# The first block's decay scalars: TensorE takes their small products behind the projections' dense products in each turn, not ahead of them

## The chip, the cores and the metric

The kernel runs on one core of a Trainium2 chip. The metric is the device time of one execution in microseconds (us), the median over timed runs; lower is better. In the rows PE is TensorE (matrix products and transposes), PEld its weight loads, DVE is VectorE, ACT is ScalarE, POOL is GpSimd and SP is SyncE, which issues the transfers.

## The reference, cut to what matters

Two blocks of two layers each work on a sequence of 512 positions and 1024 features. The change concerns the first block, in both of its layers. There a normalised input `h` is projected into attention (q, k, v), into a gated delta rule (qd, kd, vd and two sets of scalars, beta and decay, for 2 directions x 8 heads) and into gates:

```
proj = h @ w_in[l]
(qa, ka, va, qd, kd, vd, beta_logit, decay_logit, z, gate_logit) = jnp.split(proj, offsets, axis=-1)
...
y_attn = grid_attention(qa, ka, va) @ w_o_attn[l]
qkv = jax.nn.silu(centred_depthwise_conv(jnp.concatenate([qd, kd, vd], axis=-1), dn_conv_w[l])).astype(f32)
...
beta = jax.nn.sigmoid(beta_logit.astype(f32)).reshape(b, s, 2, DN_HEADS)
g = -jnp.exp(dn_a_log[l].astype(f32)) * jax.nn.softplus(
    decay_logit.astype(f32).reshape(b, s, 2, DN_HEADS) + dn_dt_bias[l].astype(f32))
o = bidir_gated_deltanet(qd, kd, vd, beta, g)
...
gcum = jnp.cumsum(g, axis=-1)
g_tot = jnp.exp(gcum[..., -1])
```

The "decay scalars" are `g`, its running sums within chunks of 64 (`gcum`) and the exponential of each chunk's total (`g_tot`).

## The kernel before, in words

Every engine has a program of its own, written out in Python: the classes `Tensor` (PE), `Scalar` (ACT), `Vector` (DVE), `Pool` and `Sync` all derive from `Program`. Each engine does its instructions strictly in the order in which its generator emits them, and waits on semaphores for events of the others. The generators of the several strands of work are interleaved by hand: `abreast(a, b, c)` takes one step of each strand in each turn, in the order in which they are given, and `beside(main, fill, 1, 1)` puts one step of `fill` behind every turn of `main`.

`Program.mixed` sets the order of the middle of a layer. Its first stage, which the change touches, interleaves four strands on each engine:

- `scalars`: the small products of the decay scalars. On PE there are three groups. The first, the *scalar transposes* (4 of 32x32, L617), turns the product of `h` with the scalars' weights. The second, the *running sums* (key `cum`, 3 products from `s_scg`), and the third, the *totals* (key `tot`, 4 products from `s_scg`, L852 to L856), work on `g`. DVE takes the first and the second, ACT the third: it writes `s_egt`, the exponential of the totals (L1592).
- `begun` and `project(0, (1,))`: the dense products of the delta rule's q, k and v, two halves each, here called q0, q1, k0, k1, v0, v1 (keys `(l, "p", 0, s3, j)`). One step on PE is half of one, 12 products of 128x512 with `s_h` and `s_whi` or `s_wlo`. On ACT and DVE each of them goes on with a convolution of five taps (ACT writes the middle one into `s_tmp`, DVE adds four more, L1974, two in one step and two in a later one), then a tanh on ACT and a product on DVE (silu). For q and k a square on ACT and a sum of squares over it on PE follow; for k and v, four transposes.
- `fill`: the attention, whose units go score (PE, `s_vtok,s_dno`), row maximum (DVE, `s_nm`), exponential (ACT, `s_x`), two sets of four transposes (PE L700), their copies (DVE and ACT write `s_ktok`) and the product with v (PE, `s_ktok,s_vtok`). The sets of transposes are numbered T0, T1, ...

PSUM has eight banks. Which bank a product takes is decided by a queue in the program, not by the chip:

```
    def take(self, key):
        buffer, free = self.slots.pop(0)
        self.after(free)
...
    def give(self, key, *free):
        buffer = (self.k.bank if isinstance(self, Tensor) else self.k.tmp)[key]
        self.slots.append((buffer, free))
```

`give` puts a bank at the end of the queue, together with the event that will free it; it is called where PE's program has issued the product, long before that event. `take` pops the bank at the head, whichever it is, and makes PE wait for its event. So the order of PE's instructions also decides which product waits for which reader of an earlier one. A dense product gives its bank with the event "last tap of the convolution", which DVE reaches late; the running sums give theirs with the event `kd0`, DVE's subtraction into `s_sckd`.

Of the kernel before, what the change touches and what calls it, by code (L numbers as in the profile page):

```python
# [176 lines left out]
class Program:  # L177
# [72 lines left out]
    def behind(self, mark):  # L250

        while self.made < min(self.k.marks.get(mark, 0) + AHEAD, len(self.k.order)):
            self.one_ahead()
# [11 lines left out]
    def mixed(self, l, attention, scalars, begun, project, gates, plug):  # L265

        units = lambda g: abreast(self.units(l, g, 0), delayed(self.units(l, g, 1), 2))  # L270
        fill = itertools.chain(attention(), project(1, (0, 1)))
        beside(abreast(scalars, begun, delayed(project(0, (1,)), 0)), fill, 1, 1)
        beside(plugged(units(0), plug, (0, 1, 4, 5, 21, 22)), fill, 1, 1)
        beside(plugged(self.chain(l, 0), plug, (0, 1, 4, 5, 8, 9, 12, 13)), fill, 1, 1)
        for _ in fill:
            pass
        fill = gates()
        beside(plugged(units(1), plug, (4, 5, 21, 22)), fill, 5, 4)
        beside(self.chain(l, 1), fill, 5, 4)
        for _ in fill:  # L280
            pass

    def gates_with(self, b, c):


        return () if b == 0 else (c,) if b == 1 else (0, 1) if c == 0 else (c + 1,) if c < 7 else ()

    def project(self, l, g, js, *inputs):

        items = [(l, "p", g, s3, j) for s3 in range(3) for j in js]  # L290
        return overlapped((self.project_begin(key, *inputs), self.project_end(key)) for key in items)
# [17 lines left out]
def together(*parts, lag=0):  # L309

    live = list(parts)
    n = 0
    while live:
        for p in list(live):
            if n < lag * parts.index(p):
                continue
            if next(p, 1) == 1:
                live.remove(p)
        n += 1


def abreast(*parts):

    live = list(parts)
    while live:
        live = [p for p in live if next(p, 1) != 1]
        yield


def beside(main, fill, n, turns):  # L330

    left = 0
    for _ in main:
        left += turns
        while left >= n:
            left -= n
            next(fill, None)
# [10 lines left out]
def plugged(steps, plug, turns):  # L348
    for n, _ in enumerate(steps):
        if n in turns:  # L350
            next(plug, None)
        yield


def delayed(steps, n):
    for _ in range(n):
        yield
    yield from steps


def overlapped(items):

    rest = []
    for head, tail in items:
        for _ in head:
            rest = [p for p in rest if next(p, 1) != 1]
            yield
        rest.append(tail)
    yield from abreast(*rest)
# [137 lines left out]
def grid_attn(m, l):  # L507
    return Attn(lambda p, e, i: m.aq[half(e), p, tile(i)], lambda p, e, n: m.ak[half(e), 0:n],
                lambda p, e, c: m.av[:, c, half(e)], lambda i: 512, False, None, m.aE, m.aPT,
                [("vec_qk", (l, "q", 4), "out")], 0, 0, each=lambda p: ("vec_qk", (l, "q", p), "out"), clear=[("dma_spill", l)], lag=1)  # L510
# [20 lines left out]
class Tensor(Program):  # L531
# [230 lines left out]
    def layer1(self, l):  # L762
        m, d = self.m, self.d
        hi, lo = m.mixh
        wt = d["w1"]
        tag = ("mix", l) if l else "in"
        ht, raw = self.normed(tag), self.unscaled(tag)

        scalars, begun = self.scalars(l, hi, lo, ht), self.project(l, 0, (0,), hi, lo, ht)

        def first(c):
            if c < 6:
                self.lin((l, "q", ORDER_Q[c]) if c < 5 else (l, "v"), wt[l, ORDER_Q[c] if c < 5 else 5], 8, m.raw[:, 0], m.raw[:, 1], raw, amid=(lambda: self.total(tag)) if c == (l == 0) else None)
            elif c == 6:
                next(scalars)
            else:
                next(begun)
                next(begun)

        def rest(c):  # L780
            if c < 5:
                self.qk((l, "q", ORDER_Q[c]), K_BO)
            elif c == 5:
                self.turned((l, "v"))
        for _ in behind(first, rest, 8, LAG):
            pass
        f, A = grid_attn(m, l), ("A", l)

        self.mixed(l, lambda: self.attention(A, f), scalars, begun, lambda g, js: self.project(l, g, js, hi, lo, ht),
                   lambda: itertools.chain(self.gates(l, hi, lo, ht), self.early(l, hi, lo, ht)),  # L790
                   self.plug(l, hi, lo, ht))

        def branch(name, c, gate, w, made, a):
            if name == "a" and c > 4:
                self.lin((l, name, "g", c), wt[l, gate + c], 8, hi, lo, ht)
                self.give((l, name, "g", c), ("act_mix", l, name, c))
            self.lin((l, name, c), d[w][l, c], 4, a[:, 0], a[:, 1], made)
            self.give((l, name, c), ("vec_mix", l, name, c))

        def branch_a():  # L800
            for c in ORDER_A:
                branch("a", c, 22, "woa", lambda k: [("vec_mix", l, "oat", k)], m.orr)
                yield

        def outputs():
            for i in range(4):
                yield
                self.to_features((l, "D"), i, m.o[:, i, :], ("vec_mix", l, "o", i), ("vec_mix", l, "gated", i))
                yield
        together(outputs(), branch_a())  # L810
        for c in range(8):
            branch("d", c, 30, "wod", lambda k: [("vec_mix", l, "od", 3)], m.odr)

        def step(c):
            self.lin((l, "o", c), d["wo1"][l, c], 8, hi, lo, lambda k: [("vec_mix", l, "h", k)])
            self.give((l, "o", c), ("vec_x", l, "mix", c))
        for c in range(8):
            step(c)
        tag = ("ffn", l)
        ht2, raw2 = self.normed(tag), self.unscaled(tag)  # L820
        act = m.ffa
        for n, (f0, nf) in enumerate(FGROUPS):
            for f in range(f0, f0 + nf):
                for half in range(2):
                    if f < RAW:
                        self.lin((l, "up", f, half), d["wup"][l, half * FT + f], 8, m.raw[:, 0], m.raw[:, 1], raw2, amid=(lambda: self.total(tag)) if f + half == 0 else None)
                    else:
                        self.lin((l, "up", f, half), d["wup"][l, half * FT + f], 8, hi, lo, ht2)
                    self.give((l, "up", f, half), ("vec_ffn", l, f, half, "conv"))

            def step(c):
                self.lin((l, "dn", n, c), d["wdn"][l, c][:, f0 * 128:(f0 + nf) * 128], nf, act[:, 0], act[:, 1], lambda k: [("vec_ffn", l, f0 + k, "lo")])
                self.give((l, "dn", n, c), ("vec_x", l, "ffn", n, c))
            for c in range(8):
                step(c)

    def scalars(self, l, hi, lo, ht):
        m, sc = self.m, self.m.sc
# [137 lines left out]
    def units(self, l, g, r):  # L976
        for jp in range(2):
            yield from self.unit(l, g, jp, r)
# [65 lines left out]
    def gates(self, l, hi, lo, ht):  # L1044
        for c in range(4):
            key = (l, "z", c)
            yield from self.lin_steps(key, self.d["w1"][l, 18 + c], 8, hi, lo, ht, 2)
            self.give(key, ("vec_proj", key))
            yield
# [1950 lines left out]
```

How the kernel before makes its waits and increments, by code:

```python
    def wait_ge(self, signal, value):  # L152
        if self.passed.get(id(signal), 0) < value:
            self.passed[id(signal)] = value
            self.e.wait_ge(signal.sem, value)
# [38 lines left out]
    def after(self, events):  # L194
        for event in events:
            self.w.wait_ge(*self.at(*event))
# [340 lines left out]
    def weights(self, key, src, kt, w=128):  # L537
        n = self.used
        self.used += 1
        if self.k.counting:
            self.k.order.append((src, kt, w))
            self.k.number[key] = n
        self.w.wait_ge(*self.at("lo", n))
        return [a[:, 0:kt * w].rearrange("p (k m) -> p k m", k=kt) for a in self.m.half[n % TILES]]
# [48 lines left out]
    def turned(self, key):  # L594
        self.give(key, ("act_attn", *key, "copy"))
        ps = self.take((key, "T"))
        self.w.wait_ge(*self.at("act_attn", *key, "copy"))
        self.turn4(ps, self.tmp((key, "s"))).then_inc(*self.up("pe_feat", *key))
        self.give((key, "T"), ("act_attn", *key))
# [1 line left out]
    def lin_narrow(self, key, src, kt, hi, lo, made, w):  # L602
# [6 lines left out]
            last = self.mm(ps[0:w, :], wlo[:, k, :], hi[:, k, :], False, k == kt - 1)  # L609
        last.then_inc(*self.up("prod", self.used - 1))
        self.give(key, ("act_dn", key, "copy"))
        yield
        ps = self.take((key, "T"))
        self.w.wait_ge(*self.at("act_dn", key, "copy"))
        s = self.tmp((key, "s"))
        for i in range(4):
# [678 lines left out]
    def raw(self, tag):  # L1295
        m = self.m
        n, col, made = self.raws(tag)
        self.w.wait_ge(*self.at("dma_par", n, "row"))
        def square(c):
```

## Time and profile before

| | |
|---|---|
| median of 3 timed runs | 3263.2 us (3262.95 to 3265.39) |
| the profiled execution's own time | 3262.69 us |
| its span, first to last instruction | 3260.8 us |
| PE busy | 3137.0 us, 96% of the span |
| mean granted TensorE clock | 0.993 of full speed |
| the changed stage, layer 0 | about 60 to 141 us of the span |
| the changed stage, layer 1 | about 1010 to 1085 us of the span |

The span is what the trace covers; the profiled execution took 1.9 us more than it, and 0.5 us less than the median of the timed runs. A row of a timeline gives the start in us, the duration in us, the engine, the line, the operation with what it writes and reads, and the number of instructions merged in the row; brackets at its end hold the idle time just ahead of it on that engine, and what ended it.

### The profile page before, as it was taken

What the parts mean: (1) busy time and instruction counts of PE and PEld (TensorE: products, weight loads), DVE (VectorE), ACT (ScalarE), POOL (GpSimd) and SP (SyncE); (2) the same over time, 40 slices, a digit from 0 to 9 for tenths busy, and PEclk for the clock granted to TensorE, in tenths of its full rate; (3) what the DMA queues carried; (4) which work ended last, traced back from release to release, by engine and by line L of the source; (5) the groups of instructions that cost most, each with busy time, mean ns of one, the idle gap of its engine ahead of it and who ended that gap; (6) DMA issues with size and microseconds to landing.
All of it is one profiled execution on the core that took longest, in us unless ns stands there. A gap on an engine that the chain in (4) does not pass through costs nothing.

```text
span 3260.8 us, 59864 instructions
## 1 busy us (share of the span) xinstructions
PE 3137.0 (96%) x25752; PEld 2483.0 (76%) x25752; DVE 1886.1 (58%) x3058; ACT 1394.3 (43%) x2454; POOL 446.7 (14%) x440
## 2 busy tenths in 40 slices
PE   8899999999999999999999999999999999999999
PEld 5687778888876687878888876777788767676887
DVE  6576657756466675656745565554444555635443
ACT  5645224434246544334433355454433454544432
POOL 0051430000000331600000002211200011203010
PEclk9899999999999999999999999999999999999999
DMA  5001103333332011123333232222132232221323
GB/s 177 27 22 47 41 29 123 106 95 97 95 116 81 21 29 54 41 71 112 97 97 96 88 122 99 62 65 72 56 94 74 89 109 69 65 72 58 86 73 100
DMA packets 80215, 255.02 MB, mean 78 GB/s; under 512 B 11344, under 2 KB 13008, under 8 KB 78928
## 3 DMA queue, kind: packets, MB, share of 16 engines
q1 hardware_dynamic: 79952, 251.19, 25.0%
q8 instruction: 204, 3.34, 0.4%
q14 instruction: 59, 0.48, 0.0%
HBM read 238.08 MB, written 6.29 MB: 75 GB/s over the span
## 4 chain that ended last, share of the span: by engine, by line
PE 79%; DVE 9%; ACT 6%; issue 2%; DMA 1%; POOL 1%; SPq 1%; ACTq 0%; DVEq 0%; POOLq 0%
PE psum L535 76%; PE psum L700 3%; DVE s_wlo L1971 2%; DVE s_xb L1971 1%; ACT s_tmp L1273 1%; ACT s_whi L1273 1%; DVE s_tmp L1974 1%; DVE s_ffy L1974 1%; DMA s_stage<-w 1%; POOL s_xb L2690 1%; ACT s_E L1273 1%; ACT L1283 1%; SPq L2838 0%; DVE psum L1971 0%; ACT L1273 0%
## 5 line engine op out<-in xcount | busy, mean ns | idle before, releaser
L535 PE MATMUL psum<-s_h,s_whi 128*128 128x512 f32 (+1 forms) x4576 | 1456.9, 400 | 21.2 <-DVE s_wlo L1971 14.3
L535 PEld LDWEIGHTS psum<-s_h,s_whi 128*128 128x128 f32 (+1 forms) x4576 | 847.2, 189 | 235.2 <-issue 34.8
L535 PE MATMUL psum<-s_h,s_wlo 128*128 128x512 f32 (+1 forms) x2288 | 897.5, 392 | 0.0
L1971 DVE TENSOR_TENSOR s_wlo<-s_stage,s_whi 128x1024 fp32r<-128x1024 f32 (+2 forms) x468 | 533.9, 1143 | 358.5 <-ACT s_whi L1273 357.4
L1273 ACT ACTIVATE s_whi<-s_stage 128x1024 fp32r<-128x1024 f32 (+2 forms) x468 | 450.6, 967 | 261.5 <-DMA s_stage<-w 75.9
L535 PEld LDWEIGHTS psum<-s_h,s_wlo 128*128 128x128 f32 (+1 forms) x2288 | 430.8, 188 | 95.1
L2690 POOL TENSOR_TENSOR s_xb<-s_xb,s_cstm 64x512 f32<-64x512 f32 x64 | 101.1, 1579 | 900.5 <-DVE s_xb L1971 896.3
L535 PE MATMUL psum<-s_ffa,s_whi 128*128 128x512 f32 x704 | 217.5, 390 | 4.6 <-DVE s_ffa L1971 4.6
L1974 DVE SCALAR_TENSOR_TENSOR s_ffy<-psum,s_pcol,s_ffy 128x511 f32<-128x511 f32 x176 | 131.7, 748 | 110.8 <-ACT s_ffy L1273 107.7
L1273 ACT ACTIVATE s_E<-psum,s_nm 128x256 f32<-128x256 f32 (+3 forms) x224 | 114.4, 515 | 186.7 <-DVE s_nm L2057 151.3
L535 PE MATMUL psum<-s_oR,s_whi 128*128 128x512 f32 (+1 forms) x640 | 183.4, 371 | 0.0
L2734 POOL TENSOR_SCALAR s_E<-s_E,s_inv 128x256 f32<-128x256 f32 (+3 forms) x96 | 98.2, 1036 | 495.2 <-DVE s_inv L2079 489.0
L535 PE MATMUL psum<-s_raw,s_whi 128*128 128x512 f32 (+1 forms) x480 | 154.2, 403 | 8.3 <-DVE s_raw L1974 8.3
L535 PEld LDWEIGHTS psum<-s_ffa,s_whi 128*128 128x128 f32 x704 | 131.7, 188 | 34.2 <-DVE s_ffa L1971 7.1
L1974 DVE SCALAR_TENSOR_TENSOR s_x<-psum,s_x 128x512 f32<-128x512 f32 x80 | 55.3, 691 | 165.0 <-PE psum L535 164.9
L1971 DVE TENSOR_TENSOR s_xb<-s_xb,psum 128x512 f32<-128x512 f32 (+1 forms) x176 | 102.4, 630 | 71.6 <-PE psum L535 71.6
L1273 ACT ACTIVATE s_tmp<-psum 128x512 f32<-128x512 f32 (+4 forms) x126 | 70.8, 562 | 170.0 <-PE psum L535 166.0
L535 PE MATMUL psum<-s_ffa,s_wlo 128*128 128x512 f32 x352 | 137.0, 389 | 0.0
L1273 ACT ACTIVATE s_ffy<-psum,s_pcol 128x512 f32<-128x512 f32 x88 | 60.5, 687 | 173.0 <-PE psum L535 157.2
L1273 ACT ACTIVATE s_xb<-psum 128x512 f32<-128x512 f32 x118 | 69.8, 597 | 139.0 <-PE psum L535 139.0
L535 PEld LDWEIGHTS psum<-s_oR,s_whi 128*128 128x128 f32 x640 | 114.4, 189 | 18.7
L535 PEld LDWEIGHTS psum<-s_xb 64*64 64x64 f32 x5632 | 104.5, 134 | 29.9 <-issue 15.0
(310 smaller groups left out, 4348.2 us busy)
## 6 DMA issues: line engine op xcount, KB each, us to landing
s_stage<-w SPq DMA_DIRECT2D x192, 512.0 KB, 3.6
s_stage<-wup SPq DMA_DIRECT2D x88, 512.0 KB, 3.6
s_stage<-wo SPq DMA_DIRECT2D x32, 512.0 KB, 3.6
s_stage<-wdn SPq DMA_DIRECT2D x32, 512.0 KB, 3.5
s_stage<-wdn SPq DMA_DIRECT2D x16, 384.0 KB, 3.1
spill<-s_x SPq DMA_DIRECT2D x2, 2048.0 KB, 8.7
s_stage<-woa SPq DMA_DIRECT2D x16, 256.0 KB, 2.6
s_x<-spill SPq DMA_DIRECT2D x2, 2048.0 KB, 8.0
```

The source lines that it names most:

```text
L535: return self.e.matmul(out, left, right, start=first, stop=last, skip_group_check=True)
L700: last = self.e.transpose(ps[:, tile(c)], f.e(U)[:, tile(c)], m.cst[:, K_ID, :])
L1273: return self.e.activation(out, src, func, **kw)
L1283: self.e.preload_act_table_set("natural_log_exp_and_others")
L1971: return self.e.tensor_tensor(out, a, b, op)
L1974: return self.e.scalar_tensor_tensor(out=out, in0=a, scalar=s, in1=b, op0=op0, op1=op1)
L2690: return self.e.tensor_tensor(out, a, b, op)
L2734: self.e.tensor_scalar(E, E, inv, None, ALU.mult).then_inc(*self.up("pool_attn", tag, "e", U))
```

## The change

Only PE's program changes. In each turn of the first stage of `mixed`, PE takes the step of `scalars` behind the steps of the two dense strands, where it took it ahead of them. The step of the attention still ends the turn. All other engines keep their order.

```diff
         fill = itertools.chain(attention(), project(1, (0, 1)))
-        beside(abreast(scalars, begun, delayed(project(0, (1,)), 0)), fill, 1, 1)
+        beside(abreast(*self.in_turn(scalars, [begun, project(0, (1,))])), fill, 1, 1)
...
+    def in_turn(self, scalars, dense):
+
+        return [scalars] + dense
...
# class Tensor
+    def in_turn(self, scalars, dense):
+
+        return dense + [scalars]
```

In both layers this moves the three small groups on PE, each behind the 12 dense products of its turn. The largest consequence for the order is at the totals. These are PE's rows there before the change, in layer 0, from the last product of attention with v ahead of them (`s_ktok,s_vtok`) on; the eight transposes of L700 are T4 and T5, the four products from `s_scg` are the totals, the rows with `s_h` are the first half of v1, and `s_vtok,s_dno` is the next score:

```order
L535 MATMUL psum<-s_ktok,s_vtok 64x128 x8
L700 MATMUL psum<-s_cst,s_x 128x128 x8
L535 MATMUL psum<-s_scg,s_csta 128x32 x4
L535 MATMUL psum<-s_h,s_whi 128x512 x2
L535 MATMUL psum<-s_h,s_wlo 128x512
L535 MATMUL psum<-s_h,s_whi 128x512 x2
L535 MATMUL psum<-s_h,s_wlo 128x512
L535 MATMUL psum<-s_h,s_whi 128x512 x2
L535 MATMUL psum<-s_h,s_wlo 128x512
L535 MATMUL psum<-s_h,s_whi 128x512 x2
L535 MATMUL psum<-s_h,s_wlo 128x512
L535 MATMUL psum<-s_vtok,s_dno 128x512 x2
```

And these are the same rows of PE after it, where the changed file's lines stand four further down (L539 for L535, L704 for L700):

```order
L539 MATMUL psum<-s_ktok,s_vtok 64x128 x8
L704 MATMUL psum<-s_cst,s_x 128x128 x8
L539 MATMUL psum<-s_h,s_whi 128x512 x2
L539 MATMUL psum<-s_h,s_wlo 128x512
L539 MATMUL psum<-s_h,s_whi 128x512 x2
L539 MATMUL psum<-s_h,s_wlo 128x512
L539 MATMUL psum<-s_h,s_whi 128x512 x2
L539 MATMUL psum<-s_h,s_wlo 128x512
L539 MATMUL psum<-s_h,s_whi 128x512 x2
L539 MATMUL psum<-s_h,s_wlo 128x512
L539 MATMUL psum<-s_scg,s_csta 128x32 x4
L539 MATMUL psum<-s_vtok,s_dno 128x512 x2
```

The totals moved from ahead of the 12 dense products to behind them. The scalar transposes and the running sums move in the same way in earlier turns.

ACT's program is the same before and after. These are its rows from the copy of T5 on (`s_ktok<-psum`), in layer 0, before the change: the totals' exponential, the middle tap of v0 (`s_tmp<-psum,s_pcol`), a cast of weights, a load of a function table, the tanh of k1, its square, another table, two exponentials of the attention and the two steps that make k1's norm from its sum of squares:

```order
L1273 ACTIVATE s_ktok<-psum 128x512
L1273 ACTIVATE s_egt<-psum 128x64
L1273 ACTIVATE s_tmp<-psum,s_pcol 128x512
L1273 ACTIVATE s_whi<-s_stage 128x1024
L1273 ACT_TABLE_LOAD
L1273 ACTIVATE s_tmp<-s_tmp 128x512
L1273 ACTIVATE s_tmp<-s_qkv 128x512
L1283 ACT_TABLE_LOAD
L1273 ACTIVATE s_x,s_rs<-psum,s_nm 128x512 x2
L1273 ACTIVATE s_tmp<-psum,s_eps 128x512
L1273 ACTIVATE s_tmp<-s_tmp 128x512
```

Nothing moved here: the totals' exponential still stands ahead of everything that follows it.

## Rows read from the trace of the kernel before

**Rows 1.** The page's busy time of each engine over the span.

```profile
PE 3137.0 (96%) x25752; PEld 2483.0 (76%) x25752; DVE 1886.1 (58%) x3058; ACT 1394.3 (43%) x2454; POOL 446.7 (14%) x440
```

**Rows 2.** Timeline of PE in layer 0, the changed stage.

```profile
63.62 0.43 PE L617 MATMUL psum<-s_cst,s_tmp 32*128 32x32 f32 x4 [0.40 <-ACT s_tmp L1273]
...
98.63 0.73 PE L535 MATMUL psum<-s_scg,s_csta 128*128 128x32 f32 x4
...
109.56 0.66 PE L700 MATMUL psum<-s_cst,s_x 128*128 128x128 f32 x4 [0.65 <-DVE s_sckd L1971]
112.15 1.45 PE L535 MATMUL psum<-s_scg,s_csta 128*128 128x32 f32 x8 [1.94 <-DVE s_tmp L1974]
...
118.66 0.72 PE L535 MATMUL psum<-s_h,s_whi 128*128 128x512 f32 x2
...
121.53 1.02 PE L535 MATMUL psum<-s_tmp,s_cst 128*128 128x512 f32 x2
...
123.51 1.09 PE L700 MATMUL psum<-s_cst,s_x 128*128 128x128 f32 x8
124.44 0.60 PE L622 MATMUL psum<-s_cst,s_qkv 128*128 128x128 f32 x4
...
128.53 0.63 PE L622 MATMUL psum<-s_cst,s_tmp 128*128 128x128 f32 x4 [2.44 <-DVE s_tmp L1974]
```

**Rows 3.** Timeline of PE in layer 1, the changed stage.

```profile
1012.33 0.43 PE L617 MATMUL psum<-s_cst,s_tmp 32*128 32x32 f32 x4
...
1042.08 0.53 PE L535 MATMUL psum<-s_scg,s_csta 128*128 128x32 f32 x4
...
1042.67 0.70 PE L535 MATMUL psum<-s_h,s_whi 128*128 128x512 f32 x2
...
1056.12 1.91 PE L535 MATMUL psum<-s_scg,s_csta 128*128 128x32 f32 x8 [1.94 <-DVE s_tmp L1974]
```

**Rows 4.** Timeline of DVE in layer 0.

```profile
78.92 0.22 DVE L1974 SCALAR_TENSOR_TENSOR s_scg<-s_schb,s_prow 128x64 f32<-128x64 f32 x1
...
110.57 1.53 DVE L1974 SCALAR_TENSOR_TENSOR s_tmp<-psum,s_pcol,s_tmp 128x511 f32<-128x511 f32 x2
```

**Rows 5.** The chain of work that ended last, from 112 us on: start, duration, what.

```profile
112.15 11.42 PE psum L535 x54
```

**Rows 6.** Timeline of ACT in layer 0, from the totals' exponential on.

```profile
113.64 0.22 ACT L1273 ACTIVATE s_egt<-psum 128x64 f32<-128x64 f32 x1 [1.49 <-PE psum L535]
...
118.38 0.63 ACT L1273 ACTIVATE s_tmp<-s_qkv 128x512 f32<-128x512 f32 x1 [1.05 <-DVE s_qkv L1974]
...
122.59 0.69 ACT L1273 ACTIVATE s_tmp<-psum,s_eps 128x512 f32<-128x512 f32 x1 [0.82 <-PE psum L535]
...
124.64 1.08 ACT L1273 ACTIVATE s_ktok<-psum 128x512 f32<-128x512 f32 x2 [0.70 <-PE psum L700]
...
127.03 0.63 ACT L1273 ACTIVATE s_tmp<-s_tmp 128x512 f32<-128x512 f32 x1
```

**Rows 7.** Timeline of DVE in layer 1, its copy of the scalar transposes.

```profile
1015.21 0.22 DVE L2226 COPY s_sckd<-psum 128x64 f32<-128x64 f32 x1
```

**Rows 8.** Granted TensorE clock: stretch, its length, PE busy, clock, DMA share, GB/s.

```profile
112.50:113.00 0.50, 0.50 (x6) 0.70 0.00 0
...
116.00:116.50 0.50, 0.50 (x3) 0.89 0.00 0
...
1054.50:1055.00 0.50, 0.00 (x0) 0.77 0.00 0
...
1061.50:1062.00 0.50, 0.50 (x4) 0.90 0.00 0
```

**Rows 9.** Timeline of ACT in layer 1, the same places.

```profile
1058.07 0.22 ACT L1273 ACTIVATE s_egt<-psum 128x64 f32<-128x64 f32 x1 [1.95 <-PE psum L535]
...
1067.48 0.69 ACT L1273 ACTIVATE s_tmp<-psum,s_eps 128x512 f32<-128x512 f32 x1 [1.29 <-PE psum L535]
...
1069.53 1.08 ACT L1273 ACTIVATE s_ktok<-psum 128x512 f32<-128x512 f32 x2 [0.70 <-PE psum L700]
```

## The prediction

> **What bounds the kernel now.** I read the page's busy times first: PE works 96% of the span [rows 1], so a change counts by the time in which PE stands still, or by work it gains or loses. Then I read PE's timeline in the changed stage and asked of each idle time what ended it. At the three moved groups of layer 0 the brackets say: 0.40 us ahead of the scalar transposes, ended by ACT's copy; none ahead of the running sums; 1.94 us ahead of the totals, ended by "DVE s_tmp L1974" [rows 2]. In layer 1 only the totals wait, again 1.94 us [rows 3]. At first sight the change hides 0.40 + 1.94 + 1.94 = 4.3 us behind dense work.
>
> The name of the releaser speaks against that. `s_scg`, the totals' input, was written by DVE at 78.92, 33 us earlier. The write into `s_tmp` that starts at 110.57 and ends at 112.10, 0.05 us ahead of the totals, is the last pair of taps of k1's convolution [rows 2, 4]: the totals wait for the *bank* in which k1 stood. T5 just ahead of them waits 0.65 us for `s_sckd` [rows 2], which it doesn't read either; that is `kd0`, the event that frees the bank of the running sums. So here the queue of banks makes PE wait, and the queue follows the order of PE's program.
>
> The third view is the chain that ended last. From 112.15 on it runs on PE for 11.42 us, the totals its first piece [rows 5]. ACT is close beside it: between the totals' exponential at 113.64 and the tanh of v0 at 127.03 it waits for PE only 0.82 and 0.70 us [rows 6]. The tanh leads to v0's silu on DVE and to v0's transposes, for which PE waits 2.44 us, to 128.53 [rows 2].
>
> **The change, part by part.** In a fixed program the banks can be followed, give by give.
>
> *Scalar transposes.* Before, they took the bank of the scalars' own product, whose event is ACT's copy, which they need anyway; q1 took the next, long free. Now q1's first half comes first and takes that bank. So PE waits the same 0.40 us at the same spot, for the same copy, and has the same 4 transposes and 12 products to do before the next score: 0. DVE gets the transposes later by the 12 products, 2.87 us by the price below. In layer 0 it has other work meanwhile; in layer 1 they end near 1012.33 + 2.87 + 0.43 = 1015.63 [rows 3], and DVE has read them at 1015.21 so far [rows 7]. The bounds are 0 and those 0.4 us; I take 0, as DVE's next step but one waits for ACT.
>
> *Running sums.* There is no wait ahead of them in either layer, and the same instructions run in another order [rows 2, 3]. DVE reads them only a turn later. I take 0; the upper bound is again their delay of 2.87, but nothing waits at that time. But the swap changes the queue: in this turn k1's bank and the running sums' bank are given one behind the other, and now in the other order.
>
> *Totals.* This is the part that counts. T5, which took the running sums' bank, now takes k1's, and so waits for the last tap, until 112.15 instead of 109.56 [rows 2]. Behind it v1's first half takes the running sums' bank, free long since, and the totals take one that an exponential has freed. So the 1.94 us don't vanish; they move ahead of T5 and join its 0.65 us there. From 112.15 on PE now has to do T5, 12 dense products and the totals before ACT gets the totals; before, it was the totals alone.
>
> The price of these at full clock: T5 is half of T6 and T7, which take 124.44 - 123.51 = 0.93, so 0.47; v1's other half takes 121.53 - 118.66 = 2.87 [rows 2]; the running sums, 6 instructions, take 1042.67 - 1042.08 = 0.59, so the totals' 8 take 0.79 [rows 3]. The sum is 4.13 us of full-clock work. But the clock is not full there. The stretch with 0.70 (0.20 us of its half microsecond at full speed, 0.30 at half) says that it fell to half, 1.2 GHz, at 112.70, the one with 0.89 that it was back at 2.4 GHz at 116.11, after PE had stood idle for 0.65 and 1.94 us and then gone back to work [rows 2, 8]. If the clock does the same again, PE does 0.55 us of the work before the fall, 3.41 / 2 = 1.70 at half clock, and the other 1.88 after: the totals end at 112.15 + 0.55 + 3.41 + 1.88 = 117.99. ACT started 0.04 us behind their end before (112.15 + 1.45 = 113.60, then 113.64 [rows 2, 6]), so `s_egt` starts at 118.03, 4.39 us later.
>
> What is queued behind it on ACT is the middle tap of v0, a weight cast, k1's tanh and square, two exponentials, k1's norm, the copy of T7, and v0's tanh; DVE's taps and silu of these hang on them. Of ACT's idle time in this piece, the 1.05 us for k1's silu are a round trip to DVE that starts from the same tap, and stay. The 0.82 for k1's sum of squares and the 0.70 for the transposes are waits for PE, which isn't late by as much, and give way [rows 6]. So v0's tanh is late by 4.39 - 1.52 = 2.87, and with it the silu and PE's wait for it at 128.53. PE itself is late by less up to there (T5's 0.47 and a new wait for k1's square); its wait takes up the rest. Behind it attention, convolution and the units of the delta rule follow from one another on all three engines, so I see nothing that gives the time back.
>
> In layer 1 the clock fell at 1054.77 and rose at 1061.60 [rows 8]. From 1056.12 on [rows 3] that is 5.48 us at half clock, 2.74 of work, then 1.39: the totals end at 1062.99, `s_egt` starts at 1063.03 instead of 1058.07, 4.96 later. ACT's waits that give way are 1.29 + 0.70 = 1.99 [rows 9]; 2.97 us remain.
>
> The sum is 0 + 0 + 2.87 + 2.97 = 5.8 us. Against the profiled execution's own 3262.69 that is 3268.5; its span and the 1.9 us around it both carry it. The median of the runs lies 0.5 higher, so I predict **3269.0**.
>
> **The unknown in it: the clock.** Bounds come from rows at either level. All 4.13 us at full clock: the totals end at 116.28 and 1060.25, the cost is 2.68 - 1.52 = 1.16 and 2.22 - 1.99 = 0.23, together 1.4, which gives 3264.6. All at half, 8.26 us: `s_egt` at 120.45 and 1064.42, cost 5.29 and 4.36, together 9.7, which gives 3272.9. I take the clock as the rows have it, as the gaps lie in the same places; T5 no longer breaks them up, so a rise is no likelier than before. Below nothing the cost can't go by the clock.
>
> The Trainium skill has a rule on this, in "TensorE: Matmul & The Clock Gate", section "HAM oscillation — how this bites in real kernels": a wait that leaves TensorE idle long enough puts the array back to half clock, and what follows starts cold. By that rule the change is a bad one, since it joins two short gaps into one, and the dense products start behind it. The trace agrees on the fall behind such gaps; were every product up to the totals cold, the time would be the 3272.9 of the bound, and otherwise the sum stands.
>
> **The rivals.**
> - *The waits vanish (faster).* If the totals waited for their data, dense work would cover 4.3 us: 3258.9, 0.13% less. It needs banks that are free at T5. For it speaks only the bare length of the brackets; against it, that DVE's event at 112.10 and not `s_scg` ended the wait, and that T5 already waits for a bank.
> - *ACT's delay is hidden, or the clock holds.* Then only T5's 0.47 us per layer remain, 3264.1, or the 1.4 us of the full clock, 3264.6. For it: PE has a 2.44 us wait later on, and ACT waits 1.49 us ahead of `s_egt` already [rows 6]. Against it: that later wait ends on the same ACT chain, and 1.52 us of slack is less than 2.87 of dense work even at full clock. It decides if `s_egt` comes less than about 2 us later.
> - *The half clock lasts (clearly slower).* 3272.9, as worked out above. In layer 1 it lasted twice as long as in layer 0 in the same program, so it can; it decides if the clock stays at half until the totals are done in both layers.
>
> **How the numbers follow.** Chances: the forecast mechanism with the clock about as before 0.60 (its own range 3266 to 3271.5); hidden or full clock 0.20; half clock throughout 0.14; waits vanish 0.06. A measurement of this kernel can tell about 0.2% from no change, 6.5 us, so the line lies at 3269.7, just above the forecast. Slower by more than that: the 0.14 of the half clock and 0.24 of the forecast's upper part, 0.38. Faster by more than that needs more than the 4.3 us of the first rival: 0.02. The other 0.60 lie within. The range from 3263.5 to 3273.0 takes in both bounds of the clock and leaves out the first rival and a little at either end.
>
> **What would show it.** In the trace after: no bracket ahead of the totals; ahead of T5 one bracket of about 0.65 + 0.66 + 1.94 = 3.2 us (T5's own row, which moves out, and the two gaps around it), ended by "DVE s_tmp L1974", and the like in layer 1; the 0.40 us now ahead of q1's first half, still ended by ACT `s_tmp`; `s_egt` with a wait of 4 to 5 us on ACT; ACT's waits for k1's sum and for the copy of T7 gone; a wait of about a microsecond ahead of k1's sum of squares on PE; v0's transposes at about 131.4 and, with layer 0's delay, 2.9 + 3.0 us later in layer 1. The prediction is wrong if T5 starts near 109.5, if `s_egt` comes less than 2 us later, or if PE's later idle times shrink by what it loses here.

## The result, and the profile after

The change makes the kernel slower: 3273.95 us (3269.02 to 3277.13, 8 runs) against 3263.81 (3260.45 to 3266.57, 8 runs), a ratio of 1.0029, 95% interval [1.0018, 1.004]. That is +9.5 us by the ratio, +10.1 by the medians. The prediction was 3269.0 with a range up to 3273.0; the median lies 0.95 us above it. The profiled execution took 3275.07 us, its span 3273.2.

The page's busy times, to compare with [rows 1]:

```profile
PE 3140.2 (96%) x25752; PEld 2484.0 (76%) x25752; DVE 1886.5 (58%) x3058; ACT 1394.1 (43%) x2454; POOL 447.3 (14%) x440
```

PE has the same instructions and 3.2 us more busy time in a span that is 12.4 us longer. So most of the loss is standing still, and the rest is work at a lower clock. Not all of it lies where the change is: of the 12.4 us this pair of traces has only 2.5 in the two changed stages (from DVE's write of `s_scg` to the first unit of the delta rule), 3.1 ahead of layer 0's, 1.9 between the layers and 4.9 behind layer 1's. How much of this belongs to the change is asked further down. The timeline of PE in layer 0 shows what moved, to compare with [rows 2]:

```profile
66.70 0.70 PE L539 MATMUL psum<-s_h,s_whi 128*128 128x512 f32 x2 [1.09 <-ACT s_tmp L1281]
...
109.68 0.66 PE L704 MATMUL psum<-s_cst,s_x 128*128 128x128 f32 x4
114.32 1.06 PE L704 MATMUL psum<-s_cst,s_x 128*128 128x128 f32 x4 [3.98 <-DVE s_tmp L1982]
115.03 1.20 PE L539 MATMUL psum<-s_h,s_whi 128*128 128x512 f32 x2
...
119.17 0.97 PE L539 MATMUL psum<-s_scg,s_csta 128*128 128x32 f32 x8
...
125.69 1.10 PE L539 MATMUL psum<-s_tmp,s_cst 128*128 128x512 f32 x2 [1.52 <-ACT s_tmp L1281]
...
133.33 0.63 PE L626 MATMUL psum<-s_cst,s_tmp 128*128 128x128 f32 x4 [3.00 <-DVE s_tmp L1982]
```

The wait ahead of the totals is gone, and T5 has one long wait for the same releaser, the last tap of k1 on DVE. Behind T5 come the 12 dense products, and only then the totals at 119.17. New are 1.52 us ahead of k1's sum of squares, and 3.00 where 2.44 stood ahead of v0's transposes. In layer 1 it is the same picture, to compare with [rows 3]; the last row is the first unit of the delta rule, which ends the stage:

```profile
1060.70 1.12 PE L704 MATMUL psum<-s_cst,s_x 128*128 128x128 f32 x4 [3.98 <-DVE s_tmp L1982]
...
1066.73 0.98 PE L539 MATMUL psum<-s_scg,s_csta 128*128 128x32 f32 x8
...
1080.90 1.09 PE L626 MATMUL psum<-s_cst,s_tmp 128*128 128x128 f32 x4 [3.00 <-DVE s_tmp L1982]
...
1094.50 1.15 PE L539 MATMUL psum<-s_cstm,s_scg 64*64 64x64 f32 x32
```

DVE's row of k1's last pair of taps, to compare with [rows 4], ends at 114.26, 0.06 us ahead of T5:

```profile
112.73 1.53 DVE L1982 SCALAR_TENSOR_TENSOR s_tmp<-psum,s_pcol,s_tmp 128x511 f32<-128x511 f32 x2
```

ACT in layer 0, to compare with [rows 6], and the totals' exponential in layer 1, to compare with [rows 9]:

```profile
120.18 0.22 ACT L1281 ACTIVATE s_egt<-psum 128x64 f32<-128x64 f32 x1 [4.17 <-PE psum L539]
...
124.92 0.63 ACT L1281 ACTIVATE s_tmp<-s_qkv 128x512 f32<-128x512 f32 x1 [1.04 <-DVE s_qkv L1982]
...
128.20 0.69 ACT L1281 ACTIVATE s_tmp<-psum,s_eps 128x512 f32<-128x512 f32 x1
...
129.45 1.06 ACT L1281 ACTIVATE s_ktok<-psum 128x512 f32<-128x512 f32 x2
...
131.83 0.63 ACT L1281 ACTIVATE s_tmp<-s_tmp 128x512 f32<-128x512 f32 x1
...
1067.76 0.22 ACT L1281 ACTIVATE s_egt<-psum 128x64 f32<-128x64 f32 x1 [5.31 <-PE psum L539]
```

The exponential waits 4.17 and 5.31 us for the totals, where it waited 1.49 and 1.95. The 1.04 for k1's silu stayed, and the waits of 0.82 and 0.70 behind it are gone. Apart from that 1.04, ACT now has work at nearly every moment from the exponential to v0's tanh.

The windows of the granted clock, with PE's busy time as the second number and the clock as the number ahead of the last two, to compare with [rows 8]:

```profile
112.70:114.30 1.60, 0.00 (x0) 0.00 (x0) 1.56 (x4) 1.10 (x2) 0.00 (x0) 1.00 0.00 0
114.30:117.70 3.40, 3.38 (x10) 2.84 (x11) 0.56 (x1) 0.60 (x1) 0.00 (x0) 0.52 0.00 0
117.70:130.00 12.30, 10.78 (x65) 7.26 (x63) 7.12 (x10) 8.69 (x15) 0.00 (x0) 0.99 0.14 43
...
1060.00:1066.70 6.70, 6.00 (x16) 4.88 (x17) 1.24 (x2) 0.81 (x2) 0.00 (x0) 0.50 0.01 4
...
1080.00:1084.00 4.00, 2.99 (x20) 2.29 (x20) 3.90 (x7) 1.17 (x3) 0.00 (x0) 0.57 0.00 0
```

Behind T5's wait the clock stood at half (1.2 GHz) for 3.4 us in layer 0, as in the prediction, and in layer 1 up to the start of the totals, where the prediction had it rise somewhat earlier. The last window, behind v0's transposes in layer 1, was not in the prediction.

### The profile page after: what moved, and what is told of

The parts are those of the page before. It is cut to its first block, busy times and chain, and to the rows that moved or that the text cites. A ratio compares the mean times of both kernels' runs of the same rounds, so it can differ in the third digit from the quotient of the medians.

```text
span 3273.2 us, 59866 instructions
## 1 busy us (share of the span) xinstructions
PE 3140.2 (96%) x25752; PEld 2484.0 (76%) x25752; DVE 1886.5 (58%) x3058; ACT 1394.1 (43%) x2454; POOL 447.3 (14%) x440
## 4 chain that ended last, share of the span: by engine, by line
PE 78%; DVE 9%; ACT 7%; issue 2%; DMA 2%; POOL 1%; SPq 1%; ACTq 0%; DVEq 0%; POOLq 0%
PE psum L539 75%; PE psum L704 3%; DVE s_wlo L1979 2%; DVE s_xb L1979 1%; ACT s_tmp L1281 1%; DMA s_stage<-w 1%; DVE s_tmp L1982 1%; ACT s_whi L1281 1%; POOL s_xb L2698 1%; SPq L2846 1%; ACT L1291 1%; DVE s_ffy L1982 1%; ACT s_E L1281 1%; ACT s_x L1281 0%; DVE psum L1979 0%
## 5 line engine op out<-in xcount | busy, mean ns | idle before, releaser
L539 PE MATMUL psum<-s_h,s_whi 128*128 128x512 f32 (+1 forms) x4576 | 1460.9, 401 | 24.0 <-DVE s_wlo L1979 15.5
L539 PEld LDWEIGHTS psum<-s_h,s_whi 128*128 128x128 f32 (+1 forms) x4576 | 849.5, 189 | 239.0 <-issue 35.7
L539 PE MATMUL psum<-s_h,s_wlo 128*128 128x512 f32 (+1 forms) x2288 | 899.3, 393 | 0.0
L539 PEld LDWEIGHTS psum<-s_h,s_wlo 128*128 128x128 f32 (+1 forms) x2288 | 432.2, 189 | 95.7
L539 PE MATMUL psum<-s_ffa,s_whi 128*128 128x512 f32 x704 | 217.4, 390 | 4.6 <-DVE s_ffa L1979 4.6
L539 PE MATMUL psum<-s_oR,s_whi 128*128 128x512 f32 (+1 forms) x640 | 183.3, 371 | 0.0
L539 PE MATMUL psum<-s_raw,s_whi 128*128 128x512 f32 (+1 forms) x480 | 154.4, 403 | 8.7 <-DVE s_raw L1982 8.3
L539 PEld LDWEIGHTS psum<-s_ffa,s_whi 128*128 128x128 f32 x704 | 131.7, 188 | 34.1 <-DVE s_ffa L1979 7.1
L539 PE MATMUL psum<-s_ffa,s_wlo 128*128 128x512 f32 x352 | 137.0, 389 | 0.0
L539 PEld LDWEIGHTS psum<-s_oR,s_whi 128*128 128x128 f32 x640 | 114.5, 189 | 18.7
L2698 POOL TENSOR_TENSOR s_tmp<-s_xb,s_cstm 128x512 f32<-128x512 f32 x80 | 117.5, 1485 | 68.6 <-PE psum L539 55.7
```

Of the source, the lines that this page charges most:

```text
L539: return self.e.matmul(out, left, right, start=first, stop=last, skip_group_check=True)
L2698: return self.e.tensor_tensor(out, a, b, op)
```

## The experiments

Differences in us below are the ratio's distance from 1 times 3264.

**The parts, one at a time.** A strand of scalars can be put last in single turns alone (turn 0 has the scalar transposes, 6 the running sums, 8 the totals):

```diff
-        beside(abreast(*self.in_turn(scalars, [begun, project(0, (1,))])), fill, 1, 1)
+        beside(self.turns(scalars, [begun, project(0, (1,))]), fill, 1, 1)
...
# class Tensor
+    LATE = (8,)
+
+    def turns(self, scalars, dense):
+        live, n = [scalars] + dense, 0
+        while live:
+            now = live[1:] + live[:1] if n in self.LATE and live[0] is scalars else live
+            done = [p for p in now if next(p, 1) == 1]
+            live, n = [p for p in live if p not in done], n + 1
+            yield
```

Totals alone, `LATE = (8,)` (x1):

> Only the totals go behind the dense products; the scalar transposes and the running sums stay ahead of them, so T5 keeps the running sums' bank and v1's first half takes k1's. If the price is ACT's totals' exponential standing ahead of its other work, the stretch from k1's first pair of taps on DVE to v0's transposes on PE grows by about 2.4 us in layer 0 and 2.5 in layer 1 (12 dense products and the totals behind the last tap, less ACT's slack of 1.5 and 2.0), and the time lies about 5 us above the kernel before. If the 10 us of the whole change come from all three moves by equal parts, it lies 3 to 4 us above; if they come from the running sums or the transposes, it is that of the kernel before.

Measured: ratio 1.0018 [1.001, 1.0027], +5.9 us. PE's timeline of this kernel in layer 0:

```profile
110.46 0.66 PE L704 MATMUL psum<-s_cst,s_x 128*128 128x128 f32 x4 [1.36 <-DVE s_sckd L1986]
...
113.15 1.00 PE L539 MATMUL psum<-s_h,s_whi 128*128 128x512 f32 x2 [2.03 <-DVE s_tmp L1989]
...
117.56 0.97 PE L539 MATMUL psum<-s_scg,s_csta 128*128 128x32 f32 x8
```

T5 keeps the running sums' bank and its own wait; k1's bank goes to v1's first half, which waits 2.03 us for the last tap. The totals come 4.4 us behind that, after the dense products, and most of the loss is there without T5's exchange. About 5 us were expected.

Running sums alone, `LATE = (6,)` (x2):

> Only the running sums go behind the dense products. The banks are swapped: T5 waits for k1's last tap, the totals follow it at once. If the price is ACT's, T5's four transposes cost PE at most 0.5 us per layer and the totals' exponential starts 0.5 us later than before, which ACT's slack hides: 0 to 1 us above the kernel before. If it is the swap of the banks itself, about as much as the whole change, 6 to 10 us.

Measured: 1.0009 [1.0, 1.0018], +2.9 us, more than expected.

Scalar transposes alone, `LATE = (0,)` (x3):

> Only the scalar transposes go behind the dense products. By my working 0 (PE waits for the same copy at the same spot, DVE has other work), within 1 us of the kernel before; if the later scalars hold up DVE or the shifted banks cost something later in the program, 2 to 4 us above it.

Measured: 1.0006 [0.9997, 1.0015], +2.0 us, not told apart from nothing.

The change, with ACT taking the totals' exponential six instructions later (the same `turns` on ACT, `LATE = (8,)`; x4):

> All of the change on PE, and in addition ACT takes the totals' exponential six instructions later (behind v0's middle tap, a weight cast, k1's tanh and square and two table loads). If the price is the instructions queued behind that exponential on ACT, nearly all of it goes: the totals are done at about 118 in layer 0 and ACT comes to the exponential near 120, so only T5's 0.5 us per layer stay, 0 to 1.5 us above the kernel before and 5 to 9 below the change. If the price is PE's own (the longer gap, the half clock, the banks), the time stays at that of the change, 3270 or more.

Measured: 1.0007 [0.9998, 1.0015], +2.3 us. In ACT's timeline nothing stands still for the totals now:

```profile
113.85 0.68 ACT L1299 ACTIVATE s_tmp<-psum,s_pcol 128x512 f32<-128x512 f32 x1
...
120.41 0.22 ACT L1299 ACTIVATE s_egt<-psum 128x64 f32<-128x64 f32 x1
...
127.41 0.63 ACT L1299 ACTIVATE s_tmp<-s_tmp 128x512 f32<-128x512 f32 x1
```

PE's order is that of the change, and T5 still waits 3.41 and 3.43 us. The time alone doesn't decide: +2.3 is not clear of the lower measurements of the change below (+3.9). The trace does. In PE's timeline v0's transposes wait 2.44 us, as before the change:

```profile
128.91 0.63 PE L626 MATMUL psum<-s_cst,s_tmp 128*128 128x128 f32 x4 [2.44 <-DVE s_tmp L2000]
```

They stand 23.03 us behind the start of k1's first taps (105.88), and 24.16 in layer 1. In two traces of the order before it is 22.75 and 24.27, in layer 1 23.67 and 23.90; in five of the change it is 25.37 to 26.33 and 25.11 to 26.57. So what the change loses up to v0's transposes runs through ACT, which stood behind the totals, and not through PE's own wait.

**Place or bank?** The loss of the running sums alone could come from their later place or from the two banks that change their order in the queue. `give` can be put off for a key by a number of other gives:

```diff
+    def give(self, key, *free):
+        super().give(key, *free)
+        if key[1:] == ("p", 0, 1, 1):
+            self.held = [1, self.slots.pop()]
+        elif getattr(self, "held", None):
+            self.held[0] -= 1
+            if not self.held[0]:
+                self.slots.append(self.held[1])
+                self.held = None
```

Running sums late, k1's bank behind theirs as before (x5):

> Of the change only the running sums' step stands last in its turn, and k1's bank is put in the queue behind theirs, so that T5 and the totals take the banks that they took before. If the +3 to +4 us of the running sums alone came from the exchange of the two banks: 0 to +1, 3264 to 3265, with T5 and the totals waiting apart again (0.6 and 1.9 us). If they came from DVE's reading the sums 2.9 us later: +3 to +4, 3267 to 3268.

Measured: 1.0004 [0.9995, 1.0012], +1.3 us. The two waits stand apart again:

```profile
109.17 0.66 PE L704 MATMUL psum<-s_cst,s_x 128*128 128x128 f32 x4 [1.39 <-DVE s_sckd L1996]
111.77 1.54 PE L539 MATMUL psum<-s_scg,s_csta 128*128 128x32 f32 x8 [1.94 <-DVE s_tmp L1999]
```

All instructions in the order before, only these two banks exchanged (the condition is `key[1:] == ("cum",)`; x6):

> The order of every instruction as before; alone the two banks are exchanged in the queue, so that T5 takes k1's bank and the totals that of the running sums. If the exchange is what costs in the running sums' part: +3 to +4, 3267 to 3268, with one wait of 4 us ahead of T5 and none ahead of the totals, and the totals done 0.5 to 1.0 us later than before. If the exchange costs only T5's own 0.5 us per layer: about +1, 3265. If the later place of the sums is what costs: 0.

Measured: 1.0002 [0.9993, 1.0012], +0.7 us. The trace shows the exchange, one wait and none ahead of the totals:

```profile
112.26 1.12 PE L704 MATMUL psum<-s_cst,s_x 128*128 128x128 f32 x4 [3.40 <-DVE s_tmp L1999]
113.17 1.76 PE L539 MATMUL psum<-s_scg,s_csta 128*128 128x32 f32 x8
```

So the place of the running sums costs nothing that shows: with the exchange, v0's transposes come 24.55 and 24.47 us behind k1's first taps where only the banks move, and 24.67 and 24.32 where the sums move too. The exchange makes the totals' exponential about a microsecond later (it starts 9.07 us behind k1's first taps, 105.89 to 114.96, where the order before has 7.86 to 8.33). ACT's slack takes up most of that in layer 0 and little in layer 1: in a second trace of the order before, v0's transposes stand 24.27 and 23.90 us behind the taps, so the exchange costs 0.3 + 0.6 us there, near the 1 us expected for T5's own time. The rest of the +2.9 of the running sums alone is no larger than what comparisons of one order of instructions differ by, as the next part shows.

**How large is the loss?** The change rebuilt with `turns` (`LATE` holds every turn), twice, on two other occasions (r1 and r2):

> The change once more, PE's order as in the changed kernel; what is asked is how large the loss is, with more runs. If the sum of the prediction holds and the rest of the first comparison was chance, +5.8 us, about 3269.6 beside a before of 3263.8. If the loss also holds what the prediction set at nothing (the running sums' exchange of banks) and a lower mean granted clock, +8 to +11, about 3272 to 3275, with a mean granted clock over its runs about 0.001 below that of before.

Measured: 1.0012 [1.0003, 1.0021], +3.9 us.

> The change a third time, since the first comparison gave +10.1 us and the second +3.9. If the prediction's sum of 5.8 us is the change's own cost and the rest is where the half clock falls in the rest of the program from run to run, +4 to +8 and a mean over the three near +6; v0's transposes again 5 to 6 us later in the two layers together, counted from k1's first taps. If the excess belongs to the change, +8 to +11 again.

Measured: 1.0012 [1.0003, 1.0021], +3.9 us.

The kernel before against itself ("before again" further down):

> The kernel before under another name, its lines moved to where the changed kernel has them, compared with itself: 0, with whatever interval; its deviation says how far a comparison of this kernel strays by itself (1 to 3 us if the half clock alone moves it). Its trace shows again how long the piece from k1's first taps to v0's transposes takes in the order before: 22.75 and 23.67 us if the first trace was typical.

Measured: 1.0005 [0.9996, 1.0014], +1.6 us for no change at all.

The changed file itself, two sets of runs beside one set of before (r4 and r5):

> The changed kernel itself, file for file, beside before on another occasion. If the change costs what the sum of the prediction says (5.8 us) and the first comparison's +10.1 was high by the occasion: +3 to +8. If the +10.1 belongs to this very file and the two rebuilt versions (+3.9 each) differ from it in something unseen: +8 to +12. In the trace the totals' exponential 12.1 to 13.4 us behind the start of k1's first taps in either case, 7.9 to 8.3 before the change.

Measured: 1.0036 [1.0023, 1.0049], +11.8 us (5 runs).

> The same file once more in the same call, for the spread between two sets of the same kernel on the same chip: within 3 us of the other set if only the half clock moves it. The second block, in which the change touches nothing, took 1321.5 to 1330.7 us in the traces of the three executions so far; it should again lie anywhere in there, with no relation to the first block.

Measured: 1.0026 [1.0016, 1.0037], +8.5 us (8 runs).

Five comparisons of the same order of instructions gave +9.5, +3.9, +3.9, +11.8 and +8.5, 7.5 us on average. The intervals of the second and third don't overlap that of the fourth. The three high ones are those of the changed file itself and the two low ones those of the rebuilt one, which is what was expected if something unseen sets the files apart. In the traces the two have the same instructions in the same order on every engine, and up to layer 1's units they take the same time: on average 1094.7 us in the three traces of the file and 1094.5 in the two of the rebuilt one. So I measured the loss in the traces as well, piece by piece. The pieces run from DVE's write of `s_scg` to k1's first taps, on to the start of `s_egt` on ACT, to v0's transposes on PE, and to the first unit; then the unit's time and the rest up to the end of the span. All are differences of the starts of rows, in us. x3 (transposes alone) and x5 (running sums alone, banks kept) have the totals and their banks as before; x4 is the change with ACT's exponential later:

```
               layer 0                      layer 1                    unit of   rest of
               taps  s_egt   v0 T  units    taps  s_egt   v0 T  units  layer 1   span
before        26.86   7.86  14.89  15.73   25.98   8.32  15.35  13.60  1087.02   2173.8
before again  25.98   7.97  16.30  13.61   25.98   8.33  15.57  13.59  1086.94   2177.8
x3            25.97   8.04  16.23  13.59   25.98   8.33  15.41  13.60  1085.80   2177.4
x5            25.98   7.95  16.33  13.60   25.99   7.49  15.23  13.60  1086.02   2174.7
after         25.97  12.23  13.15  13.59   25.97  13.43  13.14  13.60  1094.50   2178.7
r1            26.99  12.22  13.15  15.72   26.99  12.12  13.16  15.72  1096.64   2168.2
r2            26.00  13.12  13.16  14.84   27.02  12.24  13.15  13.61  1092.26   2177.5
r4            26.82  12.22  13.16  13.60   26.99  11.96  13.15  15.72  1093.44   2178.1
r5            25.97  13.18  13.15  14.88   26.91  13.26  13.14  14.92  1096.13   2177.2
x4            27.02  14.53   8.50  15.46   27.05  14.57   9.59  13.60  1090.21   2170.4
```

The reader is to see three things. Up to layer 1's units all five traces of the change are later than both of before, by 7.6 us on average. The rest of the span is the same on average (2175.9 against 2175.8), but one execution differs from another by 10 us there, although the change moves nothing in it. And several pieces come in two kinds (25.97 or about 27.0, 13.60 or 14.8 to 15.7), and the longer kind goes with the clock: the first row of each kernel below is the stretch at and behind PE's wait ahead of q1's sum of squares, the second the stretch behind v0's transposes, both in layer 1, first r4 and then before again:

```profile
1040.00:1044.00 4.00, 3.06 (x16) 1.78 (x18) 2.74 (x5) 3.80 (x7) 0.00 (x0) 0.67 0.33 120
...
1078.00:1085.00 7.00, 5.73 (x46) 4.83 (x45) 4.95 (x9) 2.64 (x7) 0.00 (x0) 0.56 0.00 0
```

```profile
1040.00:1044.00 4.00, 4.00 (x37) 3.56 (x36) 1.32 (x2) 3.97 (x8) 0.00 (x0) 1.00 0.00 0
...
1073.40:1080.60 7.20, 5.21 (x52) 3.63 (x52) 5.38 (x10) 4.07 (x9) 0.00 (x0) 1.00 0.00 0
```

Not every stretch at half clock makes its piece longer: in layer 1 of the trace after, the one between 1080 and 1084 lies right behind v0's transposes, and from there to the units it still took 13.60 us.

**With banks that are free.** In the change, k1's bank put in the queue three places later (`self.held = [3, ...]`): T5 takes the running sums' bank, v1 and the totals take banks of exponentials (f1).

> The change with k1's bank put in the queue three places later, so that T5 takes the running sums' bank, v1 and the totals take banks that exponentials have freed, and the next score takes k1's. If the loss comes from the wait for k1's last tap ahead of the dense products and the totals: T5 at about its old time, the totals' exponential at about 113.7 as before, and -1 to +1 us, 3263 to 3265. If the place behind 12 dense products costs by itself: +5, about 3269.

Measured: 0.9984 [0.9975, 0.9994], -5.2 us, a larger gain than expected. PE's timeline in layer 0, then ACT's:

```profile
109.59 0.66 PE L704 MATMUL psum<-s_cst,s_x 128*128 128x128 f32 x4 [1.41 <-DVE s_sckd L1996]
...
112.85 0.97 PE L539 MATMUL psum<-s_scg,s_csta 128*128 128x32 f32 x8
```

```profile
113.86 0.23 ACT L1298 ACTIVATE s_egt<-psum 128x64 f32<-128x64 f32 x1 [1.66 <-PE psum L539]
```

The exponential is back 8.05 us behind k1's first taps (105.81), as in the order before, and ACT's later waits for PE are gone, as in the change; the second is what the expectation had left out. v0's transposes come 21.20 us behind the taps in both layers. Once more (f3):

> The change with k1's bank put in the queue three places later, once more. -4 to -5 us against before if the first result holds; the traces give -4.0 for the pieces from k1's first taps to v0's transposes, so near -4 if nothing else moves; 0 if the first was chance.

Measured: 0.9985 [0.9976, 0.9993], -4.9 us. And the order before, with k1's bank two places later (f2):

> The order before, with k1's bank put in the queue two places later, so that neither T5 nor the totals nor v1 wait for k1's last tap. If the place of the totals ahead of or behind the dense products costs nothing once the banks are free: the same as the change with free banks, -4 to -5 us, about 3260. If the totals' exponential on ACT still sets the end: 1.5 to 1.9 us per layer better than the change with free banks, about 3257.

Measured: 0.9988 [0.998, 0.9997], -3.9 us. PE's timeline, then ACT's:

```profile
110.18 0.66 PE L704 MATMUL psum<-s_cst,s_x 128*128 128x128 f32 x4 [1.36 <-DVE s_sckd L1996]
110.67 0.98 PE L539 MATMUL psum<-s_scg,s_csta 128*128 128x32 f32 x8
```

```profile
112.67 0.21 ACT L1298 ACTIVATE s_egt<-psum 128x64 f32<-128x64 f32 x1
```

With free banks both orders beat both kernels, and the place of the totals no longer shows in the time. The exponential comes 1.8 us earlier in the order before (6.27 us behind k1's first taps), but the clock then stood at half behind v0's transposes in both layers: to the units it took 15.72 us twice, in the other two executions 14.84, 13.60, 14.79 and 15.45.

## Why the prediction was right in its mechanism and too low

**The wait for a bank: right.** The long wait moved to T5, behind the releaser that was named, and it goes away with another bank and not with another place (x5, x6, f1, f2). Its size, 3.98 us in both layers, was put at 3.2. The row of layer 0 on which I summed it was the unusual one: T5 waited 0.65 us there, but 1.36 in layer 1 of the same trace and in both layers of before again.

**Scalar transposes, running sums at nothing: not contradicted.** x3, x5 and x6 lie within 0.06% of before, each with no change at all inside its interval. The wait for ACT's copy moved ahead of q1's first half, as forecast; it is 1.09 us in the trace after for 0.40 in before, but 0.60 in before again and absent in two of the five traces of the change, so its size goes with the execution. The running sums alone (x2) measured +2.9 with an interval from 0 up; what shows of it in the pieces is the exchange of the banks, 0.3 to 0.6 us a layer.

**ACT's queue: right.** The exponential was to start 4.39 and 4.96 us later. Counted from k1's first taps, the means of five traces against two are 12.59 - 7.92 = 4.7 and 12.60 - 8.33 = 4.3. The waits that give way were put at 1.52 and 1.99; from the exponential to v0's transposes 13.15 us are left of 15.60 and 15.46, so 2.45 and 2.31. That the path is ACT's is shown by x4, where v0's transposes come as early as before although PE keeps the order of the change.

**The totals' term: mis-sized.** It was 2.87 + 2.97 = 5.8 us, and it measured 2.2 + 2.0 = 4.2, because ACT's waits in the order before give way by more than the rows said. In layer 0 the trace of before was again the odd one: 14.89 us there, 16.23 to 16.33 in before again, x3 and x5. With those two counted to before, the term is 1.9 + 2.2 = 4.1.

**The step that failed: the clock outside the piece up to the totals, put at nothing, and with it the range.** The measured median lies above the range. I took the clock "as the rows have it, as the gaps lie in the same places", and let it vary only between the release of the bank and the totals; from this came the upper end, 3273.0. The runs showed half clock in other places. In layer 1 the piece ahead of k1's taps took 26.78 us on average instead of 25.98, and the piece behind v0's transposes 14.71 instead of 13.60, together +1.9, where neither trace of before has a stretch at half clock. In layer 0 the same two pieces changed by -0.07 and -0.14, but only because the first trace of before has the longer kind of both. So the two stages cost 4.2 + 1.9 - 0.2 = 5.9 us, or 6.6 with x3 and x5 counted to before. That this is near the predicted 5.8 is luck: it is that sum out of other terms. That the longer kinds belong to the change is borne out by all sixteen traces kept: of these four pieces they are 19 of 32 in the eight traces with the full order of the change on PE (free banks among them), and 6 of 32 in the other eight. Why that order meets half clock more often there was not tested.

Outside the stages I had put nothing. By these traces 1.7 us more are lost there: 0.7 ahead of layer 0's `s_scg` (80.15 against 79.48 on average), 1.0 between the layers (880.6 against 879.5 from units to `s_scg`). Over the sixteen traces this goes away (79.85 and 880.2 in the eight with the order of the change, 79.87 and 880.5 in the other eight), so I put it down to chance. That the 7.6 of these traces is close to the 7.5 of the five timed comparisons is then luck in part, and the change's own cost is about 6 to 7 us. The recorded +9.5 lies above that and the two of +3.9 below. Of the 4.95 us between forecast and measurement, 0.6 is before's own median, 3263.8 in 8 runs for 3263.2 in 3. The range had no term for this spread, although the part of the program that the change doesn't touch varies by 10 us from execution to execution, and before strayed 1.6 us from itself. Why three sets were high and two low, with the same order of instructions, stays open: the high ones are those of the changed file and the low ones those of the rebuilt one, but as far as the chips are on record they also ran on different ones, and no run separates file, chip and chance.

**The rivals.** "The waits vanish" needed free banks, as it said, and where they were made free its 4.3 us of gain came out at 3.9 to 5.2. The agreement is luck in part: T5 still waits 1.41 us there, and the gain comes with ACT's path, not from dense work hiding the brackets. "Hidden" is refuted by the exponential's 4 to 5 us. "Half clock lasts" up to the totals in both layers was seen in no trace: `s_egt` would have stood 14.7 us behind k1's taps (7.86 + 6.81 in layer 0), and the latest stood at 13.18 there and at 13.43 in layer 1.

The Trainium skill's rule ("TensorE: Matmul & The Clock Gate", section "HAM oscillation — how this bites in real kernels"), that work behind a long idle time starts cold, speaks in the right direction. The traces agree in that each stretch at half clock shown here in the two stages lies behind or in a wait of PE. But the same wait doesn't always do it: 2.31 us ahead of q1's sum of squares were followed by a clock of 0.67 in r4 and of 1.00 in before again.

## What to carry to other kernels

Before hiding a wait behind other work, find out whether it is for data or for a buffer: a wait for a bank follows the order of the queue and moves to whatever takes that bank next, and everything that was moved behind it becomes late. Then look at who reads the moved product and what is queued behind the reader, since an engine that works in strict order passes the delay on, less what it would have waited for others on the way (here 4.7 us became 2.2). Here moving one bank three places in the queue was worth more than any order of the products that was tried.

For a loss of a quarter of a per cent, sum up the pieces of several traces as well as the timed medians, and put the spread of the untouched part of the program into the range.

## What the runs showed that I had not expected

The granted clock falls in different places in executions of one and the same order of instructions. The second part of the program, from layer 1's units to the end, took 2168.2 us in one execution of the change (r1) and 2178.7 in another (after). A window in it, behind the start of the second block, had a granted clock of 0.98 in the trace of before and of 0.90 in that of before again:

```profile
1940.00:2010.00 70.00, 61.79 (x262) 43.88 (x260) 40.35 (x77) 37.26 (x70) 13.83 (x14) 0.98 0.36 115
```

```profile
1940.00:2010.00 70.00, 61.53 (x245) 43.63 (x244) 39.19 (x72) 32.98 (x61) 13.34 (x12) 0.90 0.35 108
```

Where such a fall doesn't make it longer, a piece repeats to a few hundredths of a microsecond (25.97 to 26.00, 13.14 to 13.16, 13.59 to 13.61), so that a single trace looks far more certain than it is.
